# Feed-forward layers of a fused four-layer block: first chunk started amid the attention output products, all four accumulation banks in one layout, down products two chunks behind

## What is computed

```python
D_MODEL, SEQ, D_FF, CONV_WIDTH = 1024, 256, 2816, 3

def conv_ffn(x, w_up, conv_w, conv_b, w_down):
    hdn = x @ w_up                                  # 256 x 5632
    hdn = lax.conv_general_dilated(hdn, conv_w[:, None, :], ..., feature_group_count=2 * D_FF) + conv_b
    gate, up = jnp.split(hdn, 2, axis=-1)
    return (jax.nn.gelu(gate, approximate=True) * up) @ w_down

# in the layer loop, o being the attention output
h = h + rmsnorm(merge_heads(o) @ w_o, post_g)
f = conv_ffn(rmsnorm(h, ffn_pre_g[layer]), w_up[layer], conv_w[layer], conv_b[layer], w_down[layer])
h = h + rmsnorm(f, ffn_post_g[layer])
```

## Time and profile before

| what | value |
|---|---|
| median of 3 runs | 855.21 us (855.15 to 855.37) |
| profiled execution | 855.34 us, its span 853.5 us |
| PE busy | 843.8 us, 99% of the span |
| DVE, ACT busy | 681.0 us (80%), 513.7 us (60%) |
| last attention product to chunk 1, each layer | 119.33 to 134.88 us, and the same 302.28 us later |

### The profile page before, as it was taken

The page is one execution under the profiler, slowest core; times in us unless marked ns, Lnnn a source line. Parts: engine busy times, 40 slices in busy tenths (PEclk is TensorE's granted clock), DMA queues, the critical chain, the costliest instruction groups (busy, mean ns, idle before and its releaser), DMA issues.

```text
span 853.5 us, 14686 instructions
## 1 busy us (share of the span) xinstructions
PE 843.8 (99%) x5596; PEld 739.1 (87%) x5596; DVE 681.0 (80%) x1045; ACT 513.7 (60%) x746; POOL 58.7 (7%) x118
## 2 busy tenths in 40 slices
PE   9999999999999999999999999999999999999997
PEld 8999889888888889888898888888889889998885
DVE  6776569888887987666689878888888887699784
ACT  6665656865655683575576655656746857542552
POOL 2232100000000012200010000000000001000000
PEclk9999999999999999999999999999999999999999
DMA  8645326555546446533456465455264154462411
GB/s 338 230 163 173 127 99 228 192 203 200 188 160 233 148 171 233 215 103 145 149 212 245 151 218 205 165 184 210 100 222 149 63 188 167 151 234 75 188 50 50
DMA packets 22520, 147.71 MB, mean 173 GB/s; under 512 B 2863, under 2 KB 3151, under 8 KB 5824
## 3 DMA queue, kind: packets, MB, share of 16 engines
q1 hardware_dynamic: 20448, 140.52, 45.4%
q0 software_dynamic: 1872, 6.37, 2.2%
q10 hardware_dynamic: 144, 0.04, 0.0%
HBM read 145.86 MB, written 1.06 MB: 172 GB/s over the span
## 4 chain that ended last, share of the span: by engine, by line
PE 94%; DVE 2%; ACT 2%; issue 1%; DMA 1%; POOL 0%; POOLq 0%; DVEq 0%; SPq 0%
PE psC L2115 17%; PE psC L2028 12%; PE psC L2029 11%; PE psC L2030 11%; PE psC L2118 9%; PE psD L2028 5%; PE psD L2029 5%; PE psD L2030 5%; PE psC L2145 2%; PE psC L2147 2%; PE psC L2154 2%; PE psD L2445 1%; PE psD L2437 1%; PE psD L2855 1%; PE psD L2477 1%
## 5 line engine op out<-in xcount | busy, mean ns | idle before, releaser
L1166 DVE TENSOR_TENSOR w_lo<-raw,w_hi 128x2048 fp32r<-128x2048 f32 x122 | 279.0, 2289 | 55.7 <-ACT w_hi L583 55.1
L583 ACT ACTIVATE w_hi<-raw 128x2048 fp32r<-128x2048 f32 x125 | 238.4, 1911 | 66.6 <-PE psC L2030 32.7
L2115 PE MATMUL psC<-xT,w_hi 128*128 128x512 f32 x640 | 201.1, 396 | 0.0
L2118 PEld LDWEIGHTS psC<-xT,w_lo 128*128 128x128 f32 x640 | 120.4, 188 | 28.0
L2118 PE MATMUL psC<-xT,w_lo 128*128 128x256 f32 x640 | 125.8, 278 | 0.0
L2115 PEld LDWEIGHTS psC<-xT,w_hi 128*128 128x128 f32 x640 | 98.6, 189 | 1.3
L2028 PE MATMUL psC<-xT,w_hi 128*128 128x256 f32 x304 | 87.2, 287 | 0.1
L2029 PE MATMUL psC<-xT,w_hi 128*128 128x256 f32 x304 | 86.1, 283 | 0.0
L2030 PE MATMUL psC<-xT,w_lo 128*128 128x256 f32 x304 | 86.1, 283 | 0.0
L2028 PE MATMUL psD<-w_hi,oT_hi 128*128 128x512 f32 x208 | 81.2, 390 | 0.0
L2029 PE MATMUL psD<-w_lo,oT_hi 128*128 128x512 f32 x208 | 81.1, 390 | 0.0
(11 more groups left out here) (343 smaller groups left out, 1498.0 us busy)
## 6 DMA issues: line engine op xcount, KB each, us to landing
raw<-stream SPq DMA_DIRECT2D x130, 1024.0 KB, 4.8
gbc<-post_g POOLq DMA_DIRECT2D x6, 512.0 KB, 4.2
arena<-first SPq DMA_DIRECT2D x4, 512.0 KB, 5.1
arena<-f_rows POOLq DMA_DIRECT2D x4, 512.0 KB, 10.9
h<-x_in SPq DMA_DIRECT2D x2, 512.0 KB, 9.3
out<-h SPq DMA_DIRECT2D x3, 256.0 KB, 2.0
arena<-b_in POOLq DMA_DIRECT2D x1, 640.0 KB, 5.8
out<-h SPq DMA_DIRECT2D x2, 128.0 KB, 2.0
```

The source lines that it names most:

```text
L583: nc.scalar.activation(w_hi[:, slot, :], raw[:, raw_slot, :], ACT.Copy).then_inc(hi_done, 1)
L1166: V.tensor_tensor(w_lo[:, slot, :], raw[:, raw_slot, :], w_hi[:, slot, :].bitcast(F32), ALU.subtract).then_inc(lo_done, 1)
L2115: MM(psC[:, up_bank(e, a), :], hi[:, k, a * P:a * P + P], xT[:, kk_, :, :].rearrange("p i t -> p (i t)"), start=(kk_ == 0), stop=False, sk ...
L2118: ins = MM(psC[:, up_bank(e, a), 0:T], lo[:, k, a * P:a * P + P], xT[:, kk_, 0, :], start=False, stop=(kk_ == KT - 1), skip_group_check=True)
```

## The change

**Order of PE.** Four of the eight transposes of the first rows go before the last nine of the attention's output products (`last_pieces_turn`). `features_first` is replaced by `up_first`: chunk 0 uses all four banks in the layout of `up_wide`. Its first 16 matmuls take the first 128 rows of x, both parts, for the first four input tiles, two banks at a time; the second rows follow as matmuls of their own (128x2x128), and the second half of the inputs is done with 512 columns. The ten unused matmuls go. The spreading matmul comes at the end of chunk 0. The down product of chunk j comes after the up product of chunk j+2 instead of j+1, so the beginning is up 0, up 1, up 2, down 0, up 3, down 1.

**Order of ACT and DVE.** Four tiles of the first rows are rounded and split amid the post-norm. The squares of the second rows come after the split of the next unit. Chunk 0 goes through `lower` and `added` as the others do; the load of the gelu table comes between its two `lower`. Chunk 1 has to wait for `added` of chunk 0.

```diff
@@ ACT @@
+            def first_rows_early(n, gain):
+                for k in range(4):
+                    act.wait_ge(xT_turned, KT * TT * (n - 1) + 4)
+                    nc.scalar.activation(xT_hi[:, k, 0:P], xtile(n, k)[:, 0:P], ACT.Copy, scale=col(gain, k)).then_inc(early_x, 1)
...
                 def chunk(j):
-                    if j < NJ - 1:
-                        split_to(u0 + 3 * j + (3 if j else 4))
+                    if j == 0:
+                        lower(0, u0 + ups_done(0), (0,))
+                        act.preload_act_table_set("gelu_apprx_tanh_and_others")
+                        lower(0, u0 + ups_done(0), (1,))
+                    split_to(u0 + ready(j, 0))
                     if j:
-                        lower(j, u0 + 3 * j + (0 if j == NJ - 1 else 1))
+                        lower(j, u0 + ups_done(j))
...
@@ DVE @@
                 def chunk(j):
...
+                    if j == 0:
+                        for g in range(2):
+                            add_lower(0, g, u0 + ups_done(0))
+                        split_to(u0 + ready(0, 0))
+                        pre_spread(1 + 2 * layer)
+                        for g in range(2):
+                            scale(0, g)
+                    else:
+                        split_to(u0 + ready(j, 0))
+                        scaled(j, u0 + ups_done(j))
                     taps(j, j % 2)
...
@@ PE @@
                 def banks_free(j):
 
-                    return [(f["added"], 2 * (j - 2) + g + 1) for g in range(2)]
+                    return [(f["added"], 2 * (j - 1) + g + 1) for g in range(2)]
...
-                for j in range(1, 3):
-                    up(j, u0 + 3 * j - 1)
-                    down_peeled(j - 1, u0 + 3 * j + 1)
+                for j in range(3):
+                    up(j, u0 + 2 * j)
+                down_peeled(0, u0 + 6)
...
+            def last_pieces_turn(piece, n):
+                for c in range(2):
+                    piece(c, 0, (7,)).then_inc(rows_done, 1)
+                for c in range(2):
+                    piece(c, 1, (4, 5))
+                piece(0, 1, (6,))
+                transposes(n, 0, range(4))
+                piece(0, 1, (7,)).then_inc(unit_done, 1)
+                piece(1, 1, (6, 7)).then_inc(unit_done, 1)
...
+def ready(j, i):
+    return (3 * j + 2 + i) if j > 1 else ((4, 5, 5), (6, 7, 7))[j][i]
+def ups_done(j):
+    return 3 * j if j > 1 else 2 * j + 2
...
-    order = [ups[0, 0], ups[0, 1]]
-    for j in range(1, NJ - 2):
-        order += [ups[j, 0], ups[j, 1], downs[j - 1]]
-    order += [*ups[NJ - 2], *ups[NJ - 1], *downs[NJ - 3:]]
+    order = [*ups[0], *ups[1]]
+    for j in range(2, NJ):
+        order += [*ups[j], downs[j - 2]]
+    order += [*downs[NJ - 2:]]
```

More of the change, by code:

```diff
@@ L660, in pre, with pre_wide @@
                         split_half(SECOND[n], b - 1)
+            def first_rows_early(n, gain):
+                for k in range(4):
+                    act.wait_ge(xT_turned, KT * TT * (n - 1) + 4)
+                    nc.scalar.activation(xT_hi[:, k, 0:P], xtile(n, k)[:, 0:P], ACT.Copy, scale=col(gain, k)).then_inc(early_x, 1)
+            def pre_wide(n, gain):
+                pre_squares(n, 0)
+                for b in range(4):
+                    for k in (2 * b, 2 * b + 1):
+                        act.wait_ge(xT_turned, bank_turned(n, k))
+                        rows = slice(P if k < 4 else 0, T)
+                        ins = nc.scalar.activation(xT_hi[:, k, rows], xtile(n, k)[:, rows], ACT.Copy, scale=col(gain, k))
+                        if k == 0:
+                            ins.then_inc(first_x, 1)
+                    ins.then_inc(xT_hi_done, 1)
+                    if b > 1:
+                        split_half(SECOND[n], b - 2)
+                split_to(SECOND[n] + 2)
+                pre_squares(n, 1)
             def pre_square(n, tt, c):
@@ L700, in keys_x, with post @@
                 ins.then_inc(kv_hi_done, 1)
-            def post(i):
+            def post(i, early_gain=None):
                 for tt, c in post_steps(i):
+                    if (tt, c) == (1, 0) and early_gain is not None:
+                        first_rows_early(i + 1, early_gain)
                     act.wait_ge(*rows_wait(i, tt, c))
@@ L740, in centre, with lower @@
                         ins.then_inc(f["centre"], 1)
-                def lower(j, up_done):
-                    for g in range(2):
+                def lower(j, up_done, parts=(0, 1)):
+                    for g in parts:
                         at = up_bank(e0, 2 * g)
                         if g == 0:
-                            act.wait_ge(f["upper"], j)
+                            act.wait_ge(f["upper"], j + 1)
                         else:
@@ L1263, in pre, with first_rows_lo, pre_wide @@
                         split_half(SECOND[n], b - 1)
+            def first_rows_lo(n, gain):
+                for k in range(4):
+                    dve.wait_ge(early_x, 4 * (n // 2) + max(k, 3 if k == 2 else k) + 1)
+                    V.scalar_tensor_tensor(xT_lo[:, k, 0:P], xtile(n, k)[:, 0:P], col(gain, k), xT_hi[:, k, 0:P].bitcast(F32),
+                                           ALU.mult, ALU.subtract).then_inc(early_lo, 1)
+            def pre_wide(n, gain):
+                for b in range(4):
+                    dve.wait_ge(xT_hi_done, xt_base(n) + b + 1)
+                    for k in (2 * b, 2 * b + 1):
+                        rows = slice(P if k < 4 else 0, T)
+                        ins = V.scalar_tensor_tensor(xT_lo[:, k, rows], xtile(n, k)[:, rows], col(gain, k),
+                                                     xT_hi[:, k, rows].bitcast(F32), ALU.mult, ALU.subtract)
+                    ins.then_inc(xT_lo_done, 1)
+                    if b > 1:
+                        split_half(SECOND[n], b - 2)
+                split_to(SECOND[n] + 2)
+                pre_means(n)
             def kv_x_lo(tt, ks):
@@ L1323, in post @@
                 update(0, 1)
+                if early_gain is not None:
+                    first_rows_lo(i + 1, early_gain)
                 if i != 4:
@@ L1450, in split @@
                             split_lo(first + 6 * i, first % HL, first % RAW)
+                        split(1)
+                        scaled(j, u0 + 3 * j)
+                        taps(j, (3 + par) % 2)
                         split(2)
-                        scaled(j, u0 + 3 * j + 1)
-                        taps(j, (3 + par) % 2)
+                        product(j, (3 + par) % 2)
                         split(3)
-                        product(j, (3 + par) % 2)
-                        split(4)
                         gate_lo(j, (3 + par) % 2)
-                nsplit[0] = u0 + 3 * (NJ - 2) + 2
+                nsplit[0] = u0 + 3 * (NJ - 2) + 1
                 for j in (NJ - 2, NJ - 1):
@@ L2055, in turn @@
                     return
+                if n in (1, 3):
+                    return
                 transposes(n, 0, range(KT))
```

185 lines of the change are left out of this document (117 added, 68 removed).

## The result

The changed kernel takes 871.87 us (median of 4 runs, 871.56 to 872.23), the kernel before 855.29 us in the runs beside it. The ratio is 1.0194, with a 95% interval of 1.0176 to 1.0212: 16.6 us slower. The profiled execution took 871.92 us, and its span is 870.2 us against 853.5. The prediction was 873.2 us.

What follows compares the result with a forecast made beforehand. The prediction took PE to bound the kernel (busy 843.8 of 853.5 us). First layer -0.8 + 7.5 + 2.6 = 9.3, second -0.8 + 7.5 + 2.0 = 8.7, together +18.0 us: 873.2 us, range 870 to 876.

Steps and rivals of the forecast that it cites:

- The start, -0.8 us a layer: Layer start: chunk 1 begins at 134.1 instead of 134.9, after a 0.5 us wait; 2.1 us the most possible.
- A split operand at 0.12 us: Chunk 0's matmuls with a split moving operand (128x2x128) take 0.12 us each, as 256 columns side by side do.
- The bound of 0.23: Worst case for chunk 0's split-operand matmuls: 0.23 us each, adding 3.5 us per layer.
- The stop, 7.5 us a layer: Ahead of up 2, PE waits for DVE's first addition of chunk 1, from 145.2 to 152.7, in both layers.
- The lower bound, 3.3 us if ACT were never late: Ahead of up 2: DVE's own work from 133.4 ends the addition at 148.5, a wait of 3.3 us.
- The clock, 2.0 us, paid in the second layer only: After the wait at up 2, matmuls restart at half clock, costing 2.0 us; in the first layer up 3's wait swallows it.
- Only DVE's own work counts: Rival: ACT's splits come in time, up 2 waits 3.3 us per layer, the clock holds: 861 us; chance 0.07.
- Up 3, 2.6 us in the first layer: At up 3, ACT is late behind the sine's table loads; PE waits 0.2 and 2.4 us, together 2.6.
- The sum: Both layer starts: 9.3 us lost in the first layer, 8.7 in the second, together +18.0 us, giving 873.2 us.
- third one of 2.4 us: Sign in PE's wait list: besides two waits on DVE's addition, one of some 2.4 us on a remainder, once.
- PE was to be busy 2 to 4 us less: Sign in the new profile: PE's busy time falls by about 2 to 4 us.
- the one in which the clock holds (871.2): Rival: after the wait at up 2 the clock does not fall, or recovers at once; 2.0 us less, chance 0.18.

Runs made afterwards that it cites:

- The start put in order: New start with down units one chunk behind as in the kernel before, ACT's and DVE's queues rearranged (squares, mean and diagonals earlier, splits moved): 855.05 us, ratio 0.9995.
- the last experiment: Changed kernel's unit order (down units two chunks behind) on the new start with rearranged ACT and DVE queues and one split cut in four: 861.64 us, ratio 1.0076.
- the order alone: Kernel before with its old start, but the changed kernel's unit order (down units two chunks behind) and its waits: 866.78 us, ratio 1.0133.
- The last two experiments: New start, ACT and DVE queues rearranged, one split cut in four: down units one chunk behind, 853.98 us; two chunks behind, 861.64 us.
- the order alone, with its split back: Old start with down units two chunks behind, split of unit 4 again behind chunk 0's product and gelu as in the kernel before: 863.57 us, ratio 1.0096.
- the start alone: Changed kernel's new start, but down units one chunk behind, with order, waits and units as in the kernel before: 860.14 us, ratio 1.0052.
- the run with the additions ahead: Changed kernel with chunk 1's two additions, and ACT's lower halves for them, ahead of chunk 0's product, gate_lo and the split of unit 5: 867.01 us, ratio 1.0133.

## Why the prediction was right

It forecast the side, the place and the mechanism, and came out 1.3 us high, because two terms were too long (the stop by 0.4 us a layer, up 3 by 0.5). By its own steps:

- **The start, -0.8 us a layer.** Right: PE waits 0.47 us for the diagonals and chunk 1 begins 0.78 us earlier. The gap for the transposes is closed as described: the first eight matmuls of chunk 0 come at 119.73. The start put in order shows that the prediction's reason was the right one. With the squares and diagonals ahead it gives 1.34 us, of the 2.1 that the prediction called the most.
- **A split operand at 0.12 us.** Right: eight of them take from 119.73 to 120.68, 0.12 each. The bound of 0.23 is out.
- **The stop, 7.5 us a layer.** The chain was right link by link, and 0.4 us too long: 7.1. Chunk 0's scaling ended at 140.0, as forecast. The product was forecast behind a remainder ending at 146.5 and started at 146.16. The 3.6 us from the earlier trace rows for the taps include 0.1 us that DVE waits for their end before the product. With a remainder behind them nothing waits. The experiments split the 6.9 us of idle time: 2.0 us that the order makes with the old start, 1.7 us from the place of one split, and the rest, 3.2 us, from the new start.
- **The lower bound, 3.3 us if ACT were never late.** DVE's waits for ACT in the chain are 0.33, 1.04, 0.56, 0.70 and 1.11 us, 3.7 together, and that is what lies between 3.3 and 7.1. Putting one split back took away the last two and no more. In the last experiment none of the five is left, and PE waits 0.99 and 0.41 us at up 2. That is below the 3.3, because DVE's own work stands in another order there too: the split of unit 5, 2.2 us, comes behind chunk 1's first addition. So 3.3 was a bound for this one order of DVE's queue, and not for the order of the units.
- **The clock, 2.0 us, paid in the second layer only.** Right in kind. It measured 1.8 us in either layer of the profile. The traced run with 56 matmuls in the stop shows that removing it gives 1.7 us in the second layer and nothing in the first; the three untraced ones do not show the gain, and the four with the sine moved gain in both layers. What was wrong is the use of the 4.3 us from the earlier trace rows, in the rival "Only DVE's own work counts", as a length below which the clock holds: it fell in both layers behind stops of 3.7 us (the order alone) and 2.0 us (44 matmuls).
- **Up 3, 2.6 us in the first layer.** The most mis-sized term, by 0.5 us. The slow matmuls and what remains at up 3 together are 2.1 us (1.84 and 0.31). With 56 matmuls in the stop it is up 3 alone, which takes 2.1 us longer behind a wait of 1.77; of the wait of 0.2 at its first half there is none. The cause, the sine and its tables on ACT, is shown by moving them.
- **The sum.** First layer -0.8 + 7.1 + 2.1 = 8.5 (9.3 forecast). Second layer -0.8 + 7.1 + 1.8 = 8.1 (8.7 forecast). Together 16.6, and the span grew by 16.7.

Two signs named at the prediction's end were wrong. The list of waits has no third one of 2.4 us, because the slow matmuls of up 2 cover it. And PE was to be busy 2 to 4 us less, and is 2.4 us more: the slow matmuls count with 3.6 us, which the sign had left out. The rest of that difference was not traced.

None of the rivals came true. The nearest was the one in which the clock holds (871.2). Its time is close by chance, closer than the forecast's own, because the stop and up 3 were forecast too long: the clock did fall. What the order costs with the queues of DVE and ACT arranged for it was not in the prediction, which costed one arrangement. The last two experiments put it at 6.9 us in their traced runs and 7.7 in the medians.

## What to carry to other kernels

Work that stands between a producer and the engine that evacuates it is cover. Before moving it away, add up what the evacuating engines have queued until the bank is free again, and ask which of their waits it was hiding. If the order has to change, move the neighbours' queues with it: one split in another place was worth 1.7 us, and the same start was worth 4.7 us of loss or 1.4 us of gain by the order on DVE and ACT alone (one split cut in four with it). A gap moved out of one wait is only gained if no later unit asks for the same engine.

## What was not expected of the hardware

The granted clock can fall after PE is already busy again. With 44 matmuls in the stop it fell 1.4 us after the restart, 3.4 us after the matmuls had stopped. It is not a matter of length alone. Waits of 2.0 us (the order alone, with its split back) and of 2.3 to 2.4 (the start alone) were followed by a fall in one layer and not in the other, and in the run with the additions ahead the clock held through 3.22 us of waiting and fell behind the next wait of 1.81:

```profile
175.00:176.00 1.00, 0.84 (x5) 1.00 0.00 0
176.00:177.00 1.00, 1.00 (x7) 0.65 0.87 164
```

In the layer starts of these profiles no wait up to 1.5 us was followed by a fall. Where the wait was 3.7 us (the order alone) or 5.1 and more, both layers of the profile had one. A fall cost 1.5 to 2.6 us, most often 1.6 to 1.8. The Trainium skill ("TensorE: Matmul & The Clock Gate", section "What's actually happening") says that the number of slow matmuls at a kernel's start differs from run to run of the same kernel. No run here counts them there. What varies here is whether a fall comes at all: the runs of the start alone are two pairs 1.6 us apart, at mean granted clocks of 1.000 and 0.998.
